# Experts' weights in ten quarter-weight buffers instead of four half-weight buffers

## The reference, cut to what matters

```python
def mixer_block(u, cos, sin, w_in, conv_w, q_norm_g, k_norm_g, w_conv_out, w_attn_out, w_o):
    proj = u @ w_in
    cb, cc, cx, q, k, v, gc, ga = split_columns(proj)
    y_conv = (cb * depthwise_conv_centred(cc * cx, conv_w)) @ w_conv_out
    y_attn = bidirectional_gqa(q, k, v) @ w_attn_out        # after norms and rope
    merged = jax.nn.sigmoid(gc) * y_conv + jax.nn.sigmoid(ga) * y_attn
    return merged @ w_o
...
# experts: tokens sorted by expert, then for each expert e on its rows xg
#   hmid = silu(xg @ w1[e]) * (xg @ w3[e])      w1, w3: 64 x 1024 x 512
#   y    = (hmid @ w2[e]) * weight              w2:     64 x 512 x 1024
```

## Time and profile before

| what | value |
|---|---|
| median of 3 runs | 2143.91 us |
| the three runs | 2138.19, 2143.91, 2144.11 us |
| the profiled execution's own time | 2139.4 us |
| its span in the trace | 2137.7 us |
| mean granted TensorE clock | 0.908 |
| HBM read | 550.79 MB |

### The profile page before, as it was taken

How to read it: one execution, slowest core, us unless ns; L and a number is a source line. 1 busy time by engine, 2 the same in 40 slices (tenths; PEclk the granted TensorE clock), 3 DMA queues, 4 the chain that set the end, 5 groups by cost and what they waited for, 6 DMA issues and landing times.

```text
span 2137.7 us, 21061 instructions
## 1 busy us (share of the span) xinstructions
PE 1752.3 (82%) x9244; PEld 1042.6 (49%) x9244; DVE 592.8 (28%) x1394; ACT 264.1 (12%) x695; POOL 11.5 (1%) x35
## 2 busy tenths in 40 slices
PE   8989899899999999866667666666667665899888
PEld 6665566655478887512222222212223221468765
DVE  0365332754432411510111111111111110115652
ACT  0232212321102100100100000000000000112210
POOL 0000000000000000000000000000000000000000
PEclk9999999999999999988888978888887878999989
DMA  9422244238443334799999999999999999554100
GB/s 331 132 79 100 79 158 152 85 138 236 164 158 119 118 118 158 295 421 421 422 421 420 421 421 420 421 420 421 421 421 421 421 421 414 178 186 158 40 1 20
DMA packets 126582, 553.34 MB, mean 259 GB/s; under 512 B 6320, under 2 KB 8880, under 8 KB 77328
## 3 DMA queue, kind: packets, MB, share of 16 engines
q1 hardware_dynamic: 125632, 548.81, 65.4%
q0 software_dynamic: 848, 3.05, 0.4%
HBM read 550.79 MB, written 1.05 MB: 258 GB/s over the span
## 4 chain that ended last, share of the span: by engine, by line
PE 56%; DMA 34%; DVE 6%; ACT 2%; issue 1%; SPq 0%; DVEq 0%; ACTq 0%
PE bank L621 33%; DMA ring<-in_w 19%; DMA arena<-in_w 15%; PE bank L630 5%; PE bank L1070 5%; PE bank L1093 3%; PE bank L1051 2%; PE bank L609 2%; PE bank L841 1%; DVE arena L1909 1%; ACT arena L1434 1%; PE bank L667 1%; PE bank L833 1%; PE bank L772 1%; PE bank L752 0%
## 5 line engine op out<-in xcount | busy, mean ns | idle before, releaser
L621 PE MATMUL bank<-arena,ring 128*128 128x256 f32 x1856 | 417.7, 384 | 2.7 <-DVE arena L2733 2.2
L621 PE MATMUL bank<-ring,arena 128*128 128x512 f32 (+5 forms) x1000 | 380.1, 535 | 15.2 <-ACT arena L1366 3.0
L1070 PE MATMUL bank<-ring,arena 128*32 128x512 f32 x1536 | 245.3, 795 | 177.1 <-DMA ring<-in_w 152.7
L621 PEld LDWEIGHTS bank<-arena,ring 128*128 128x128 f32 x1856 | 353.9, 193 | 55.4 <-issue 7.3
L621 PEld LDWEIGHTS bank<-ring,arena 128*128 128x128 f32 x1000 | 186.8, 198 | 181.8 <-issue 151.2
L1070 PEld LDWEIGHTS bank<-ring,arena 128*32 128x32 f32 x1536 | 57.0, 141 | 361.9 <-DMA ring<-in_w 188.8
L1051 PE MATMUL bank<-arena 128*128 128x128 f32 x512 | 126.4, 419 | 29.8 <-DVE arena L2445 28.8
L1051 PEld LDWEIGHTS bank<-arena 128*128 128x128 f32 x512 | 123.4, 336 | 44.1 <-DVE arena L2445 42.0
L1070 PE MATMUL bank<-arena 128*32 128x512 f32 x512 | 81.4, 787 | 56.5 <-DMA arena<-in_w 56.5
L630 PE MATMUL bank<-arena,ring 128*64 128x256 f32 x1024 | 112.7, 380 | 0.0
L1093 PE MATMUL bank<-ring,arena 128*32 128x512 f32 x768 | 88.2, 605 | 14.3 <-ACT arena L1631 10.1
(11 more groups left out here) (368 smaller groups left out, 1230.8 us busy)
## 6 DMA issues: line engine op xcount, KB each, us to landing
ring<-in_w SPq DMA_DIRECT2D x72, 4096.0 KB, 33.7
arena<-in_w SPq DMA_DIRECT2D x24, 4096.0 KB, 35.0
ring<-in_w_in SPq DMA_DIRECT2D x42, 2048.0 KB, 7.9
ring<-in_w_out SPq DMA_DIRECT2D x6, 2048.0 KB, 7.9
ring<-in_w_ada SPq DMA_DIRECT2D x6, 2048.0 KB, 7.9
ring<-in_w_out SPq DMA_DIRECT2D x16, 512.0 KB, 9.9
ring<-in_w_conv_out SPq DMA_DIRECT2D x2, 2048.0 KB, 7.8
ring<-in_w_attn_out SPq DMA_DIRECT2D x2, 2048.0 KB, 7.7
```

Of the source, the lines that this page charges most:

```text
L621: i = te.matmul(ps, lhsT, rhs, start=n0 + k == 0, stop=n0 + k == n - 1)
L1070: m = te.matmul(ps[32 * j:32 * j + 32, :], LM.xg[:, f, 128 * k + 32 * j:128 * k + 32 * j + 32], w4[:, j, c, :], start=k == 0, stop=k == 7)
```

## The change

- A unit is now a quarter of a weight: 2.1 MB, 128 partitions x 4 experts x 1024 floats, in 4 KB pieces. There are 192 units and ten buffers (`NU = 10`): six single ring slots and four parts of the arena (`LM.early` three, `LM.late` one). Unit u waits until unit u - 10 has been used.
- The first ten units are no longer issued behind all of the mixer's loads. Units 0 and 1 go out when the mixer's attention is done on three engines (new mark `att2`), ahead of the two `wo2` loads; units 2 to 9 follow as the conv branch's buffers and the ring blocks `yc`, `ya`, `wo2` come free.
- To make room, the mixer's arrays (`L2`) and the experts' small arrays (`LM`) have new offsets, the arena grows to 25240 floats, and `hm`, `hT`, `yy`, `SwT` become single. ScalarE therefore waits for TensorE's last reader in the group before (`behind`).
- The ring no longer skips one slot ahead of the mixer (`turn[0] += 1` is gone), so the mixer's blocks lie one slot lower.
- The layer-norm rows `lng`, `lnb` of the first block get a place of their own and are loaded earlier in each layer. The scratch for GpSimd's DMAs is halved to 4096 bytes.
- The number of matmuls, their shapes and their order are the same.

```diff
-        unit_sem = [sem(f"unit{i}_loaded") for i in range(4)]
+        unit_sem = [sem(f"unit{i}_loaded") for i in range(10)]
-        AR = 22848
+        AR = 25240
-            lng, lnb = ar(15408, 1024), ar(16432, 1024)
+            lng, lnb = ar(22848, 1024), ar(23872, 1024)
...
-            hm = ar(6144, 2, 512)
-            hT = ar(7168, 2, 512)
-            yy = ar(8192, 2, 1024)
...
-            pairs = (1, 2, 0)
-            ubuf = [ring[:, 2 * p:2 * p + 2, :].rearrange("p a n -> p (a n)") for p in pairs] + [ar(14440, 8192)]
+            early = [ar(8208, 4096), ar(12304, 4096), ar(0, 4096)]
+            late = ar(4112, 4096)
+            NU = 10
+            hm = ar(21008, 512)
+            hT = ar(21520, 512)
+            yy = ar(23056, 1024)
...
-            turn[0] += 1
...
+            def unit(u, buffer=None):
+
+                if buffer is not None:
+                    ubuf.append(buffer)
+                else:
+                    s.wait_ge(*at.of("used", ("unit", u - LM.NU)))
+                g, name, q = u // 12, ("w1", "w3", "w2")[u % 12 // 4], u % 4
+                w4 = src[name][0, 4 * g:4 * g + 4].rearrange("j (p c) n -> p j (c n)", p=128)
+                le.dma_start(ubuf[u % LM.NU].rearrange("p (j n) -> p j n", j=4),
+                             w4[:, :, 1024 * q:1024 * q + 1024]).then_inc(*units[u % LM.NU].inc())
+                at.put(("w", ("unit", u)), units[u % LM.NU].sem, units[u % LM.NU].n)
+
+            def ring_unit(u, name):
+
+                s.wait_ge(*at.of("used", name))
+                users[slot_of[name]] = ("unit", max(n for n in range(12 * NG0) if n % LM.NU == u))
+                unit(u, ring[:, slot_of[name], :])
+
             for name, w in (("yc", w_conv_out_2), ("ya", w_attn_out_2), ("wo2", w_o_2)):
                 wv = w[0].rearrange("(c p) n -> p c n", p=128)
                 for g in range(2):
+                    if (name, g) == ("wo2", 0):
+                        for w in at.all(("att2", "PE"), ("att2", "DVE"), ("att2", "ACT")):
+                            s.wait_ge(*w)
+                        for u in range(2):
+                            unit(u, LM.early[u])
                     load((name, g), (whole, wv[:, :, 512 * g:512 * g + 512]))
...
+            s.wait_ge(*at.of("mm", "cb", 7))
+            s.wait_ge(*at.of("z", 7))
+            unit(2, LM.early[2])
+            ring_unit(3, ("yc", 0))
+            ring_unit(4, ("yc", 1))
+            s.wait_ge(*at.of("ev", "yc", 7))
+            unit(5, LM.late)
+            for u, name in enumerate((("ya", 0), ("ya", 1), ("wo2", 0), ("wo2", 1)), 6):
+                ring_unit(u, name)
...
                 def up(f, w):
                     ps = take(w, "w13", w)
-                    for half in range(2):
-                        name, v = unit(2 * w + half)
-                        w4 = v.rearrange("p j (c n) -> p j c n", c=4)
-                        t.wait_ge(*at.of("ev", *tag("xg", half)))
-                        for c in range(4):
+                    for q in range(4):
+                        name, v = unit(4 * w + q)
+                        w4 = v.rearrange("p j (c n) -> p j c n", c=2)
+                        t.wait_ge(*at.of("ev", *tag("xg", q // 2)))
+                        for k in (2 * q, 2 * q + 1):
                             for j in range(4):
...
-                        m.then_inc(*(t.done("mm", *tag("w13", w)) if half else t.step()))
+                        m.then_inc(*(t.done("mm", *tag("w13", w)) if q == 3 else t.step()))
                         t.also("used", name)
...
+                behind("mm", "hT")
+                se.activation(LM.hm, P[0][:, :], ACT.Tanh, scale=0.5).then_inc(*a.done("ev", *tag("w13", 0)))
...
-                ready(("mm", "pT", ly, 3, 3), *[("ev", "pv", ly, 3, g) for g in range(4)])
+                ready(("mm", "k", ly, 0), *([("h", 0, 0), ("h", 0, 1)] if ly else []))
```

More of the change, by code:

```diff
@@ L246, in program @@
         behind_group = {4: 16, 6: 17, 8: 18, 10: 19}
-        over = {g: {n: sem(f"over{g}_{n}") for n in ("pe", "dve", "act", "u0", "u1", "u2", "u3")}
+        over = {g: {n: sem(f"over{g}_{n}") for n in ("pe", "dve", "act", *(f"u{i}" for i in range(10)))}
                 for g in range(NG0, NG)}
         ring = sb("ring", [128, NR, 4096])
-        AR = 22848
+        AR = 25240
         arena = sb("arena", [128, AR])
@@ L370, in program @@
[L370 to L383, removed]
@@ L528, in further_blocks @@
                                for j in range(4)]
-                    slot4 = [Slot(o[f"u{i}"]) for i in range(4)]
-                    n = 0
-                    for name in ("w1", "w3", "w2"):
-                        for half in range(2):
[L533 to L545, removed]
+                    over_slots = [Slot(o[f"u{i}"]) for i in range(LM.NU)]
@@ new lines, in further_blocks @@
+                    for n in range(12):
+                        name, q = ("w1", "w3", "w2")[n // 4], n % 4
+                        i = (u + n) % LM.NU
+                        so.wait_ge(*(at.of("used", ("over", g, n - LM.NU)) if n >= LM.NU else
+                                     at.of("used", ("unit", u - LM.NU + n))))
+                        for j in range(4):
+                            if not at.counting:
+                                w1e = src[name][0, bass.ds(ids[j], 1)].rearrange("o (p c) n -> p (o c n)", p=128)
+                                le.dma_start(ubuf[i].rearrange("p (j n) -> p j n", j=4)[:, j, :],
+                                             w1e[:, 1024 * q:1024 * q + 1024]).then_inc(over_slots[i].sem, 16)
+                            over_slots[i].n += 16
+                        at.put(("w", ("over", g, n)), over_slots[i].sem, over_slots[i].n)
@@ L546, in further_blocks @@
                     for w in at.all(("over", g, "PE"), ("over", g, "DVE"), ("over", g, "ACT")):
                         so.wait_ge(*w)
-            u = 0
             for g in range(NG0):
[L551 to L558, removed]
+                for u in range(12 * g, 12 * g + 12):
+                    if u >= LM.NU:
+                        unit(u)
@@ L559, in sync_program @@
                 if g in behind_group:
[L560 to L564, removed]
+                    further_blocks(g, behind_group[g], 12 * g + 12)
             wv = w_in_3[0].rearrange("(c p) n -> p c n", p=128)
@@ L938, in mixer_attention @@
                             m.then_inc(*t.done("mm", "pv2", qb, hd))
+                t.also("att2", "PE")
                 yield
@@ L1114, in experts @@
             def experts():
-                parts = [expert_steps(te, t, ("unit", g), 6 * g) for g in range(NG0)]
+                parts = [expert_steps(te, t, ("unit", g), 12 * g) for g in range(NG0)]
                 mixer_rank()
@@ L1124, in experts @@
                         parts[g + 1][0](1 - f)
-                    mid_T(f)
-                    down(f)
+                    mid_T()
+                    down()
                     scatter(f)
@@ L1143, in further_blocks @@
                     to = Lane(te, over[g]["pe"], at)
-                    gather, up, mid_T, down, scatter = expert_steps(te, to, ("over", g), 6 * after + 6)
+                    gather, up, mid_T, down, scatter = expert_steps(te, to, ("over", g), 12 * after + 12)
                     gather(f)
@@ L1655, in further_blocks @@
                     ao.wait_ge(*at.of("group", after, "DVE"))
-                    expert_steps(se, ao, after % 2, ("over", g), None)
+                    expert_steps(se, ao, after % 2, ("over", g), None, None)
                     ao.also("over", g, "ACT")
```

154 lines of the change are left out of this document (77 added, 77 removed).

## The result

| | before | changed |
|---|---|---|
| median, 5 runs each | 2143.91 us | 2159.87 us |
| runs | 2138.19 to 2145.11 | 2150.37 to 2162.67 |
| profiled execution / its span | 2139.4 / 2137.7 us | 2160.9 / 2159.2 us |

The changed kernel takes 1.0071 times as long, 95% interval 1.0043 to 1.0098: slower by 16.0 us on the medians and by 21.5 us between the two profiled executions (that of the kernel before lies 4.5 us under its median, that of the changed kernel 1.0 us above).

What follows compares the result with a forecast made beforehand. The prediction took the expert stage to be bound by the DMA rate of its weight loads. Last landing +10.6 us, tail -2.6, sum +8.0: 2151.9 on the median, given as 2151 us, range for 8 in 10 2129 to 2172.

Steps and rivals of the forecast that it cites:

- More bytes before the line: Before the expert stage's steady weight loads: ten buffers, full in time, hold 21.0 MB instead of 16.8; gain 10.0 us.
- The line begins earlier: At the expert stage's first hand-back: a buffer is free after 16 records instead of 32; gain 1.5 us.
- The slope: In the expert stage's steady loads: 4 KB pieces move 411 GB/s instead of 421, 5.132 us a unit instead of 5.01.
- C: Rival for the expert loads: a piece costs nothing, rate 421 GB/s, -14.1 us, 2130; chance 0.12.
- The tail: Behind the last unit's landing: 16 records left instead of 32, taking 2.7 us; gain 2.6 us, bounds 2.0 and 3.5.
- At nothing: Extra TensorE waits, single work buffers, SyncE's 96 more issues, layer-norm rows and the like: all put at no cost.
- B: Rival for the expert loads: a piece costs little, 414 GB/s holds in the row, +1.3 us, 2145; chance 0.26.
- D: Rival for the expert loads: a row of small loads does worse (389 GB/s), +60 us, 2204, or half; chance 0.07.
- E: Rival in the expert stage: TensorE becomes the bound, its clock staying at 1.2 GHz, +38 us; chance 0.03.
- F: Rival ahead of the expert stage: a wait holds the early units until the mixer's end, +5 us more; chance 0.02.

Runs made afterwards that it cites:

- e3: The changed kernel with eight buffers instead of ten (the third and fourth arena buffer left out): 2171.46 us.
- e1: The changed kernel with each unit holding half a weight of two experts, in 8 KB pieces, buffers and number of DMAs kept: 2133.25 us.
- e2: The kernel before, with each unit's one DMA of 8 KB pieces cut into two DMAs of 4 KB pieces: 2169.27 us.
- e5: The kernel of e4, but the last w2 in quarter units of four experts (4 KB pieces), 16 records behind the last landing: 2120.75 us.
- e4: The changed kernel with each unit the whole weight of one expert, in 16 KB pieces, four units waited for and handed back together: 2124.69 us.
- e8: The kernel of e4, but quarter units in the first group's w1 and w3 and in the last w2: 2111.99 us.

## Why the prediction came out as it did

The direction was right, by the step that was meant to decide (the slope). The size was half: +8.0 forecast, +16.0 on the medians (+21.5 between the profiled executions, of which 5.7 are the start and the third block), and 2159.9 lies inside the wide range but above the 2147 to 2158 of the likeliest case. By its steps:

1. *More bytes before the line*: right. Ten units in by 876, forecast 874, the difference being the later end of the mixer; nothing moves from there to 889. e3 prices two of them at 10.3 us in the traces, as expected before it ran.
2. *The line begins earlier*: right. The issue of unit 10 was forecast at 887.8 and seen at 889.40, with a mixer that ended 1.6 us later. The unit landed 8.2 us after its issue instead of 7.8 (counted back: 1831.19 - 181 x 5.158 = 897.6), +0.4 us.
3. *The slope*: right in kind, **under-sized**. 411 GB/s was taken between the straight line's 410 and the 414 of two loads that ran alone; the row of loads runs at 409, a unit takes 5.158 instead of 5.132 us (with the late last landing of step 4 in it; 5.153 without), and over 181 units that is +4.7 us. The term was mis-sized by the weight given to the 414: the single loads were not evidence for a row, as the 2 KB rows had said. e1 and e2 show that the size of the pieces alone makes the slope (421 and 409 under the same count of DMAs), which settles rival C.
4. *The tail*: **wrong**, -2.6 forecast, +0.1 measured (12.44 against 12.35 us). This is the step whose mechanism failed. The records were halved, but TensorE ran them at 1.2 GHz (granted 0.50) and the scatter behind them at a granted 0.66. The 16 records took 3.64 us, over the bound of 3.3, which came from rows only mostly at the lower clock, and 0.9 more than the 2.7 taken. The work behind them was left out of the sum as unchanged, and its scatter took 1.8 us more. The last unit also lands 5.9 us after the one before it, where 5.1 was assumed; that is in the slope's term.
5. *At nothing*: held as far as the stage shows. (One reading there was off: the tenth slice of the earlier trace rows has a DMA share of 8 tenths, which is near full; nothing hung on it.) SyncE does stand in its queue, which the 0.37 us per issue did not foresee. The profile says of line 555 before and of line 511 after

```profile
L555 SPq DMA_DIRECT2D ring<-in_w x72: 367/370/3873, 806.9 to 1767.8; - x72
...
L511 SPq DMA_DIRECT2D ring<-in_w x114: 367/4917/11269, 794.7 to 1796.0; - x114
```

   (min/median/max ns of one issue): a median of 4.9 us where the old ones took 0.37. It costs nothing in rate, since e1 stands in its issues nearly as long, 4.6 us, at 421 GB/s.

The sum with the measured terms: 8.0 + 0.4 + 4.7 + 2.7 = 15.8 us. Both mis-sized terms erred to the same side, so the direction did not depend on luck between them.

**Rivals.** B (414 holds in the row) and C (421) fall with the 409; D (389 or holes) too. E falls because TensorE was busy for 607.01 of 912 us, at 0.86 of the clock, and its waits before products name DMA. F falls because the early units went out at 759.85.

Two statements of the Trainium skill, DMA: Bandwidth & Descriptors, were weighed. The 408.7 GB/s that its section "iDMA fabric — 4 AXI ports for 8 engines, asymmetric across TPBs" gives for a stream with 4 KiB rows agrees with the 409 of this stage; the estimate from it was +15.8 at the last landing, where 15.7 was measured. The overhead of about three bus cycles per packet, in its section "Why small descriptors are slow (HBM only)", gave an estimate of 416 GB/s; this is too little a loss here, for e1 and e2 have 421 and 409, 2.9% between them and not 1.2%.

## What to carry to other kernels

In a stage whose DMA share is full, look at the contiguous run of each transfer before its buffers: more and earlier buffers give their bytes once, a smaller run costs on every byte. If a buffer must be small, cut the weight along another axis (fewer experts, whole rows) so that the run stays long, and use the small units only where they pay: at the first hand-back and behind the last landing, where the clock can take the gain away again (12.4 us in the changed kernel, 8.9 in e5, for the same 16 records and scatter). Price a row of transfers from rows of transfers, and not from one that ran alone.

## What the runs showed of the hardware

- **A fixed loss per piece.** Rates in full rows of loads: 389 (2 KB), 409 (4 KB), 421 (8 KB), 427 GB/s (16 KB, e4). Per engine that is 84.2, 160.2, 311.3 and 613.9 ns a piece (16 x bytes / rate). From 8 to 16 KB it grows by 302.6 ns, 36.9 ns per 1000 bytes, and what is left over is 8.6, 8.9, 8.7 and 8.7 ns at the four sizes. The last two are equal by the working, and the rates are rounded to whole GB/s (one more or less at 427 moves the 8.7 by 1.4 ns), so the finding is a straight line through four sizes with about 9 ns a piece beside the bytes. e4's expectation was worked out from 4 and 8 KB alone and gave 614 ns and 427 GB/s, which both came out. In e4 the pieces of a unit follow each other in memory without a gap, in the others they don't, and the line is the same; that speaks for the pieces themselves and against scattered rows. The number of DMAs (96 or 192) doesn't show.
- **A full share says little about the rate.** It reads 1.03 at 409 and 1.01 at 427 GB/s.
- **SyncE stands in its issues when many pieces are outstanding.** Median us per issue: 0.37 with four units of 512 pieces (before), 0.43 with ten of 128 (e4), 4.6 with ten of 256 (e1), 4.9 with ten of 512 (the changed kernel). The number of transfers doesn't decide it: e4 has as many as e1.
- **The clock at the end of a stage that waits on loads.** The same 16 records took 3.64 us in the changed kernel and in e3, 1.92 in e5 and 3.17 in e8, after waits of 3.99, 4.20, 3.18 and 3.04 us. What decides it was not tried.
